# A two-model kernel on one core: gate columns in fours, one weighted sum for two norms, thirteen head products in one sequence

## The reference

```python
hc = modulate(rms_norm(ctx, norm1_g[l]), csh1, csc1)
s_ctx = bidir_delta_state(kc, vc, betac, gcx)          # 8 heads, from hc @ w_in[:, :STATE_COLS]
hx = modulate(rms_norm(x, norm1_g[l]), sh1, sc1)
y, _ = token_mixers(hx, s_ctx, w_in[l], *mix_w)        # gated delta heads + chunk MLP
x = x + gt1 * y
hx2 = modulate(rms_norm(x, norm2_g[l]), sh2, sc2)
x = x + gt2 * conv_ffn(hx2, rows, w_up[l], ffn_conv_w[l], ffn_conv_b[l], w_down[l])
...
return rms_norm(x, final_g)
```

```python
hx = _rmsnorm(x, norm_g) * (1.0 + scale_x) + shift_x
hc = _rmsnorm(ctx, norm_g) * (1.0 + scale_c) + shift_c
px = hx @ w_in
qa = _rmsnorm(hs(a_q, NA_HEADS), q_norm_a)             # each head block has its own norm
qb = _rope_2d(_rmsnorm(hs(b_q, GQA_Q_HEADS), q_norm_b), pos_row, pos_col)
...                                                     # two attentions, merge, w_out
x_new = x + gate_x * out_x
```

## Time and profile before

| | |
|---|---|
| median of three runs | 3165.26 us (3161.78 to 3167.76) |
| the profiled execution, its own time | 3160.77 us |
| span of its trace | 3159.1 us |
| PE / DVE / ACT / POOL busy | 3004.3 / 1037.8 / 727.2 / 222.5 us |
| mean granted TensorE clock | 0.981 |

### The profile page before, as it was taken

The page is one execution under the profiler, slowest core; times in us unless marked ns, Lnnn a source line. Parts: engine busy times, 40 slices in busy tenths (PEclk is TensorE's granted clock), DMA queues, the critical chain, the costliest instruction groups (busy, mean ns, idle before and its releaser), DMA issues.

```text
span 3159.1 us, 41656 instructions
## 1 busy us (share of the span) xinstructions
PE 3004.3 (95%) x16950; PEld 1726.2 (55%) x16950; DVE 1037.8 (33%) x2035; ACT 727.2 (23%) x1436; POOL 222.5 (7%) x280
## 2 busy tenths in 40 slices
PE   6999999999999999999988998999999999999998
PEld 2777767676444444444434556665555544675443
DVE  1555554554312224445211125531101212452011
ACT  3334433332200002212003224530000022362000
POOL 0222211111000000000000101000000000100000
PEclk8999999999989999999999999999999999999999
DMA  5000000002324333444331210001111112101222
GB/s 186 28 27 23 28 28 28 28 22 91 131 73 132 127 106 120 159 149 150 93 98 37 70 40 28 2 21 47 54 46 47 53 60 70 41 1 47 73 73 73
DMA packets 59846, 214.05 MB, mean 68 GB/s; under 512 B 6401, under 2 KB 8577, under 8 KB 59442
## 3 DMA queue, kind: packets, MB, share of 16 engines
q1 hardware_dynamic: 42512, 153.11, 15.3%
q0 software_dynamic: 13344, 50.59, 4.9%
...
## 4 chain that ended last, share of the span: by engine, by line
PE 90%; DVE 5%; ACT 2%; issue 2%; DMA 1%; POOL 0%; ACTq 0%; DVEq 0%
PE psum L338 87%; PE psum L704 2%; DMA arena<-in_ctxT 1%; DVE arena L1314 1%; DVE arena L1579 0%; DVE arena L1297 0%; DVE arena L1294 0%; POOL arena L1726 0%; DVE arena L1302 0%; DVE arena L1565 0%; ACT arena L942 0%; DMA arena<-in_ctx2T 0%; ACT arena L1105 0%; PE psum L534 0%; DVE psum L1571 0%
## 5 line engine op out<-in xcount | busy, mean ns | idle before, releaser
L338 PE MATMUL psum<-arena 64*64 64x64 f32 (+7 forms) x16150 | 2908.9, 363 | 143.2 <-ACT arena L875 18.4
L338 PEld LDWEIGHTS psum<-arena 128*128 128x128 f32 (+4 forms) x16150 | 1639.5, 162 | 1392.3 <-issue 1184.3
L1424 DVE SCALAR_TENSOR_TENSOR arena<-arena 128x1024 f32<-128x1024 f32 x128 | 149.3, 1221 | 4.5 <-DMA arena<-in_mods 4.4
L1672 DVE SCALAR_TENSOR_TENSOR arena<-arena,psum 128x512 f32<-128x512 f32 x32 | 21.3, 686 | 381.4 <-PE psum L338 381.4
L1105 ACT ACTIVATE arena<-psum,arena 128x512 f32<-128x512 f32 (+2 forms) x160 | 115.5, 728 | 61.3 <-DVE arena L1571 24.8
L1164 ACT ACTIVATE arena<-psum 128x512 f32<-128x512 f32 x32 | 19.1, 598 | 382.2 <-PE psum L338 382.2
L1532 DVE COPY arena<-psum 128x512 f32<-128x512 f32 (+1 forms) x26 | 18.0, 692 | 252.7 <-PE psum L338 252.7
L704 PE MATMUL psum<-arena 128*128 128x128 f32 x704 | 97.1, 282 | 2.9 <-ACT arena L1105 2.8
L704 PEld LDWEIGHTS psum<-arena 128*128 128x128 f32 x704 | 77.2, 143 | 30.6 <-issue 24.7
L1746 POOL DMA_DIRECT2D arena<-in_bias x16 | 8.8, 552 | 1193.3 <-DVE arena L1543 896.5
L1740 POOL DMA_DIRECT2D arena<-in_mods x76 | 40.3, 530 | 686.1 <-DVE arena L1424 686.1
...
## 6 DMA issues: line engine op xcount, KB each, us to landing
arena<-in_stream SPq DMA_DIRECT2D x288, 512.0 KB, 3.6
arena<-in_mods POOLq DMA_DIRECT2D x80, 512.0 KB, 3.7
...
```

The source lines that it names most:

```text
L338: return pe.matmul(out, lhsT, rhs, start=start, stop=stop, skip_group_check=True)
L1424: m = stt(mjunk[:, b % 2, :] if x < len(conds) - 1 else slot, slot, 0.5, cb[:, c, :], ALU.mult, ALU.mult, accum_out=dst(x))
```

## The change

1. **Front.** The first norm's squares go to a buffer of their own (`first_sq`); DVE adds them up (`sqsum`), and PE sums over partitions once, behind t = 13. PE waits for x and the context (`x_in`) ahead of t = 2. The gate columns are made in two groups of four tiles, first the four products of 512 columns, then the four of 256, with steps 0 to 2 of the k product behind the first group and step 3 behind the second. The first head's q product moves ahead: step 0 behind the `gcum` products, the rest behind the gate transposes. Some results change PSUM bank.
2. **Between the models.** Behind each down product DVE keeps two sums: of the squares times (final_g^2 + eps), in `sqb`, and of the plain squares, in `plain_sum`. From the first, with eps^2 in place of eps, comes the product of both roots; H is made at once from the X that is not yet normalised, with final_g in the gain (`gmod`). The second context is loaded right after the delta heads, squared by ACT in one instruction and reduced by one DVE instruction, ahead of the down products' first result. The plain root follows from one PE sum ahead of head product 1, and X is scaled by it (`last_norm`, now one tile behind each of heads 0 to 7).
3. **Heads.** All thirteen products form one sequence, each sum behind the next product; the last (`head_sum(12)`) and `rotate(3)` stand behind half of L_VB, whose context half now goes to bank 2. The wait for all rotations moves from the attention's start to the first unit that reads them.

```diff
+        plain_root = sqb[:, 0, 0:SEQ]
+        ctx_sq = flat2(mring)[:, 0:KT * CTX].rearrange("p (k n) -> p k n", k=KT)
...
                 if n in STREAMED:
-                    pe.wait_ge(s("sqsum"), (KT + 1) * (STREAMED[n] + 1))
+                    pe.wait_ge(s("sqsum"), SUMS[n])
                     m = mm(psum[:, banks[0], 0:SEQ], ones, sqb[:, 1, 0:SEQ])
                     if wide:
                         m = mm(psum[:, banks[1], 0:CTX], ones, sqb[:, 1, SEQ:TOK])
                     m.then_inc(s("nsum"), 1)
-                    return
-                for k in range(KT):
-                    norm_step(n, k, banks)
-
-            def norm_step(n, k, banks):
-
-                pe.wait_ge(s("nsq"), KT * SQUARED[n] + k + 1)
-                mm(psum[:, banks[0], 0:SEQ], ones, sqb[:, k % 2, 0:SEQ], k == 0, k == KT - 1)
-                m = mm(psum[:, banks[1], 0:CTX], ones, sqb[:, k % 2, SEQ:TOK], k == 0, k == KT - 1)
-                m.then_inc(s("nsum" if k == KT - 1 else "sq_read"), 1)
...
             for t in range(16):
                 k, hf = divmod(t, 2)
+                if t == 2:
+                    pe.wait_ge(s("x_in"), 32)
                 w = weights(pe, T_PRE + t)
                 for j in range(2):
                     r = 32 * (2 * hf + j)
                     m = mm(psum[r:r + 32, 0, :], condp[:, k, :], w[:, SEQ * j:SEQ * (j + 1)], k == 0, k == KT - 1)
                 m.then_inc(s("used"), 1)
-                if 6 <= t < 6 + KT:
-                    norm_step(0, t - 6, (1, 2))
+                if t == 13:
+                    norm_sums(0, (1, 2), True)
...
-            for k in range(KT):
-                pe.wait_ge(s("H"), k + 1)
-                r = 32 * (k % 4)
-                mm(psum[r:r + 32, 5, :], wba[:, k, :], H[:, k, 0:SEQ], k < 4, k >= 4)
-                m = mm(psum[r:r + 32, 6, 0:CTX], wba[:, k, :], H[:, k, SEQ:TOK], k < 4, k >= 4)
-            m.then_inc(s("front"), 1)
-            steps(T_HEAD, range(0, 1), 0, 1, 0)
+            for hf in range(2):
+                pe.wait_ge(s("H"), 4 * hf + 4)
+                for k in range(4 * hf, 4 * hf + 4):
+                    r = 32 * (k % 4)
+                    mm(psum[r:r + 32, 5, :], wba[:, k, :], H[:, k, 0:SEQ], k < 4, k >= 4)
+                for k in range(4 * hf, 4 * hf + 4):
+                    r = 32 * (k % 4)
+                    m = mm(psum[r:r + 32, 6, 0:CTX], wba[:, k, :], H[:, k, SEQ:TOK], k < 4, k >= 4)
+                if hf:
+                    m.then_inc(s("front"), 1)
+                steps(T_HEAD, (range(0, 3), range(3, 4))[hf], 0, 1, 0)
...
-            steps(T_HEAD, range(1, KT), 0, 1, 0)
+            steps(T_HEAD, range(4, KT), 0, 1, 0)
...
+            steps(T_HEAD + 1, range(0, 1), 4, None, 0)
             pe.wait_ge(s("gc"), 2)
...
             m.then_inc(s("gcum"), 1)
+            steps(T_HEAD + 1, range(1, KT), 4, None, 0)
...
                 if i:
                     pe.wait_ge(s("oln"), i)
-                steps(T_HEAD + 1, range(KT), 4, None, i)
+                    steps(T_HEAD + 1, range(KT), 4, None, i)
...
                 def scores(u):
                     p, q, b = us[u]
+                    if (p, q, b) == (PAIRS, 0, 0):
+                        pe.wait_ge(s("b2_rd"), 10 * l + 10)
...
+                    if u == 0:
+                        pe.wait_ge(s("b2_rs"), 5 * l + 5)
...
-                norm_sums(3 + l, (0, 1), True)
+                if l:
+                    norm_sums(4, (0, 1), True)
...
-                def heads_group(i, both):
-
...
-                            product(T0 + L_QK + j, H, 2 * (j % 2), 2 * (j % 2) + 1 if both else None, i, 4)
-                        if j:
-                            pe.wait_ge(s("b2_hsq"), 13 * l + 4 * i + j)
-                            pe.wait_ge(s("b2_hrn"), 13 * l + 4 * i + j - 1 + FREE)
-                            m = mm(psum[:, 4, :], halfones, hsq[:, (j - 1) % 2, 0:SEQ])
-                            if both:
-                                m = mm(psum[:, 5, 0:CTX], halfones, hsq[:, (j - 1) % 2, SEQ:TOK])
-                            m.then_inc(s("b2_hsum"), 1)
...
+                def head_sum(n):
+
+                    pe.wait_ge(s("b2_hsq"), 13 * l + n + 1)
+                    pe.wait_ge(s("b2_hrn"), 13 * l + n + FREE)
+                    m = mm(psum[:, 4, :], halfones, hsq[:, n % 2, 0:SEQ])
+                    if wide or n in CTX_HEADS:
+                        m = mm(psum[:, 5, 0:CTX], halfones, hsq[:, n % 2, SEQ:TOK])
+                    m.then_inc(s("b2_hsum"), 1)
+
+                for n in range(13):
+                    pe.wait_ge(s("b2_raw"), 13 * l + max(n - 1, 0) + FREE)
+                    if n == 1:
+                        pe.wait_ge(s("b2_va"), CH * l + CH)
+                        if l == 0:
+                            pe.wait_ge(s("sq"), PRODUCTS[2] + 2 * KT)
+                            mm(psum[:, 6, :], ones, plain_sum).then_inc(s("nsum"), 1)
+                    product(T0 + L_QK + n, H, 2 * (n % 2), 2 * (n % 2) + 1 if wide or n in CTX_HEADS else None)
+                    if n:
+                        head_sum(n - 1)
+                    if n >= 10:
+                        rotate(n - 10)
 
                 w = weights(pe, T0 + L_VB)
+                pe.wait_ge(s("b2_raw"), 13 * l + 12 + FREE)
                 for c in range(CH):
-                    if c == XC:
-                        pe.wait_ge(s("b2_hrn"), 13 * l + 13 + FREE)
+                    if c == 3:
+                        head_sum(12)
+                        rotate(3)
                     for k in range(KT):
-                        m = mm(psum[:, 7, (c % 4) * P:(c % 4 + 1) * P] if c < 4 else
-                               psum[:, 5, (c % 4) * P:(c % 4 + 1) * P], H[:, k, c * P:(c + 1) * P],
+                        m = mm(psum[:, 2 if c >= XC else 7, (c % 4) * P:(c % 4 + 1) * P], H[:, k, c * P:(c + 1) * P],
                                w[:, k * P:(k + 1) * P], k == 0, k == KT - 1)
                 m.then_inc(s("used"), 1)
                 rotate(4)
                 pe.wait_ge(s("b2_raw"), 13 * l + 13 + FREE)
                 pe.wait_ge(s("b2_vb"), l + 1)
-                pe.wait_ge(s("b2_qk"), 13 * l + 13 + FREE)
-                pe.wait_ge(s("b2_rd"), 10 * l + 10)
+                pe.wait_ge(s("b2_hrn"), 13 * l + 13 + FREE)
...
+            for k in range(KT):
+                if k >= 2:
+                    act.wait_ge(s("sqsum"), k)
+                f(first_sq[:, k % 2, :], X[:, k, :], ACT.Square).then_inc(s("nsq"), 1)
...
             act.wait_ge(s("ob"), HEADS + FREE)
+            act.dma_start(X[:, :, SEQ:TOK], a_ctx2).then_inc(s("b2load"), 16)
             act.dma_start(lnrows, a_lnrows.to_broadcast([P, 2, D])).then_inc(s("mixload"), 16)
...
-
+            act.wait_ge(s("b2load"), 16)
+            act.wait_ge(s("biased"), 3)
+            f(ctx_sq, X[:, :, SEQ:TOK], ACT.Square).then_inc(s("nsq"), 1)
             act.wait_ge(s("xd"), 8 + 4)
             act.dma_start(con2, a_con2).then_inc(s("b2load"), 16)
-            act.dma_start(X[:, :, SEQ:TOK], a_ctx2).then_inc(s("b2load"), 16)
...
+            norm_root(2, (0, 1), True, eps=vec("eps", 5))
...
+                if l == 0:
+                    norm_root(3, (6, None), False, to=plain_root)
+                for n in range(13):
+                    head_norm(l, n, KQ[:, n:n + 1, :] if n < 8 else bqk[n - 8])
...
+                at, done = SUMS[2] - KT, PRODUCTS[2]
+                xk, x2, gain = X[:, bass.ds(k, 1), 0:SEQ], sqb[:, 0, 0:SEQ], fgain[:, bass.ds(k, 1)]
+                dve.wait_ge(s("sqsum"), k + at)
+                dve.wait_ge(s("sq"), 2 * k + done)
+                tt(x2[:, None, :], xk, xk, ALU.mult).then_inc(s("sq"), 1)
+                dve.wait_ge(s("sq"), 2 * k + done + 1)
+                stt(sqb[:, 1, 0:SEQ], x2, gain, sqb[:, 1, 0:SEQ], ALU.mult, ALU.add).then_inc(s("sqsum"), 1)
+                tt(plain_sum, plain_sum, x2, ALU.add).then_inc(s("sq"), 1)
...
+            squares_begin(0)
+            for k in range(KT):
+                dve.wait_ge(s("nsq"), k + 1)
+                dve.wait_ge(s("sqsum"), k + 1)
+                tt(sqb[:, 1, :], sqb[:, 1, :], first_sq[:, k % 2, :], ALU.add).then_inc(s("sqsum"), 1)
...
+            tt(fgain, vec("final", 0, 8), vec("final", 0, 8), ALU.mult).then_inc(s("gate"), 1)
+            dve.wait_ge(s("gate"), 3)
+            ts(fgain, fgain, EPS, None, ALU.add).then_inc(s("gate"), 1)
+            gain_times_scale(2, vec("norm_2", 0, 8), adaT[:, 8:16, :])
+            tt(gmod[:, :, 0:1], gmod[:, :, 0:1], vec("final", 0, 8)[:, :, None], ALU.mult).then_inc(s("gmod"), 1)
             squares_begin(2)
+            dve.memset(plain_sum, 0.0)
+            dve.wait_ge(s("nsq"), KT + 1)
+            dve.wait_ge(s("sqsum"), SUMS[2] - KT - 1)
+            dve.tensor_reduce(sqb[:, 1, SEQ:TOK], ctx_sq.rearrange("p k n -> p n k"), AX_X, ALU.add)\
+                .then_inc(s("sqsum"), 1)
+            dve.wait_ge(s("gate"), 4)
...
```

(22 more changed lines are left out.)

155 lines of the change are left out of this document (49 added, 106 removed).

## The result

The changed kernel takes 3112.98 us (median of 4 runs, 3104.24 to 3118.22), the kernel before 3166.51 us (4 runs, 3161.78 to 3168.1). The ratio is 0.9831 with a 95% interval of 0.9805 to 0.9856: faster by 53.5 us, 1.7%, clear of the noise. The profiled execution has a span of 3102.4 us and a time of 3104.24, the shortest of its four. Against 3159.1 us of span before that is -56.7, where the sum of the prediction said -54.8.

The account below looks back on a forecast made before the run. PE was taken as the bound, busy 3004.3 of 3159.1 us. The terms -10.2 - 2.5 - 21.3 + 0.9 - 18.5 - 3.2 sum to -54.8, giving 3110.5 us from the median, own range 3105 to 3116 (chance 0.62).

Parts of the forecast that it names:

- A: Front: last modulation slot ends at 41.8 instead of 51.98 us, x landing at about 21; -10.2 us, bounds -13 and -0.4.
- the prediction's own signs of being wrong: Front: among these signs, slots more than 1.5 us apart behind 28 us.
- The rule weighed there: Front: PE waiting for a DMA before each small tile falls to low clock each time; -0.4 instead of -10.2 us.
- B: From T0 (DVE's first scaling of H) to the first head's kk: -2.5 us, ends 0 and -4.4.
- The new wait of 4.2 us: First head: with q moved from behind the decay rows, PE stalls 4.2 us for ACT's squares of k.
- C: Between the models, last down product to first value product: -21.3 us, ends -19 and -23.
- The plain sum: Head stage: costs PE one matmul, +0.9 us; its root and eight scalings fit behind the products.
- D: Heads: 13.4 us of PE gaps and 3 x 1.7 us of clock loss go; -18.5 us, ends -16.5 and -18.5.
- E: Attention's start: PE starts scores about 2 us earlier; -1.6 us a layer, -3.2 in all, ends 0 and -3.2.
- The clock did not hold: Rival: no half clock before the first kk or behind the gaps between the models; another -5 to -8, 3104; chance 0.14.
- the stream rival: Front: PE stays at half clock through the slots, or x lands late; gain only -0.4, so 3120 us; chance 0.15.
- The slots did not wait one at a time: Front rival: 14 slots taken singly at 5.7 us, the last ending at 101; sum +4, 3170 us; chance 0.02.

Follow-up runs that it names:

- d_groups: Changed kernel with the sums of heads 3 and 7 directly behind their own products again, in both layers: 3128.3 us.
- bias_full: Changed kernel with the mixer's row bias added by a product over all 128 partitions instead of one: 3097.93 us, ratio to the kernel before 0.9792.
- heads_only: Kernel before with the head sequence and the later attention waits alone, no plain sum: 3139.04 us, ratio to the kernel before 0.9923.
- att_wait: Changed kernel with PE held at each attention's start until the last rotated block is written, as before: 3115.86 us.
- no_plain: Changed kernel without the plain norm's work (PE sum, root, scalings) in the heads of layer 0: 3117.25 us.

## Why the prediction was right

The time, 3110.5, is 2.5 us from the median of 3112.98, and the span, 3104.3, is 1.9 us from 3102.4. Term by term, it was less exact than that:

- **A, the slots: -10.2 forecast, -7.5 measured,** and -7 to -9.5 over the executions with these slots. The landing of x (21, measured 22.0) was right, and so were the half clock behind the long wait and the hidden squares and additions. The step that was off: "Behind them the DMAs set the pace: 0.52 MB at 0.4 MB/us is 1.31 us a slot". The windows from 27 to 45 have 336, 239 and 309 GB/s, so ten slots took 27.70 to 44.49, 16.8 us instead of 13.8 (ten at 1.31 are 13.1, not the 13.3 written). That is 1.68 us a slot, and more than 1.5 was one of the prediction's own signs of being wrong: it came. About 1 us of the difference is the clock, since `d_groups` and `bias_full`, back at full pace by 32 us, end their last slot at 43.59 and 43.42; what held the stream for the rest stays open. A second size was off without effect: at half clock four slots took 3.64 us, not 2.0 each, but the next slot had not landed. The rule weighed there (the Trainium skill, "TensorE: Matmul & The Clock Gate", section "HAM oscillation") is about waits longer than the work between them. Without the wait PE waited 0.24 to 0.68 us ahead of each of the slots 9 to 13, less than the 1.05 us of a slot, and kept a granted clock of 1.00 from 21 to 33 us; the low clock in the changed kernel followed the single wait of 13.26 us.
- **B, to the first kk: -2.5 forecast, -1.1 measured, and no gain shown.** The new wait of 4.2 us on the square of k came at 4.26 and where it was said. But both ends of the forecast were mis-sized: the chain gave T0 + 52.7 for before, where the profile has T0 + 54.0, and T0 + 50.8 to 51.1 for the change, where it has T0 + 52.9. The lower clock was underrated at both (0.54 from 84 to 94 in the earlier trace rows, 0.79 from 85 to 100 in the changed kernel), and since `heads_only` passes the old order in 50.9, the 1.1 is within what the clock does from one execution to the next.
- **C, between the models: -21.3 forecast, -22.0 measured.** The value product comes 9.32 us behind the last down product, 9.0 forecast. The 1 us taken off for the clock behind C's gaps was not needed: a window at 0.56 follows (1646 to 1652), but one at 0.68 stood behind the old gap too.
- **The plain sum: +0.9 forecast, +1.0 measured** by leaving its work out. ACT's root and DVE's scalings are hidden.
- **D and E, heads and attention: -18.5 - 3.2 = -21.7 forecast.** The two layers' gain of 20.9, with the plain sum's 1.0 put back, is 21.9, and 23.2 if layer 1 is taken with the clock at its start that the kernel before had. The runs part the 23.2: 15.9 for the sums at the group ends, with the price of 1.7 us of clock behind each 2.75 measured as 1.8 in layer 0; 5.2 for the attention's start; 2.1 left for the last head's gaps of 1.89 and 1.32.
- **What the sum had no term for:** 4.57 us in the mixer, where the profiled execution of the changed kernel had the best case of a clock that varies between executions. Without it the span would have been 3107, and its median run is indeed 9 us longer than the profiled one. That the single number came out within 2 us owes something to this cancelling the 4.1 us that A and B fell short. That is luck: what was forecast well are C, D and E, which make 43 of the 54.8.

The other outcomes did not come. The clock did not hold (0.50 to 33 us). The stream was slower than forecast, but far from the 3120 of the stream rival. The slots did not wait one at a time: the largest wait of PE for a slot was 2.02 us.

A part of the rest is the clock too: from layer 1's first transposes to the end the changed kernel takes 433.6 us and the kernel before 435.8; `bias_full` and `att_wait` have 433.5 and 433.3, `no_plain` 436.3 with the same instructions there. The difference stands in the first 12 us: the granted clock is 1.00 there in the changed kernel and 0.72 in `no_plain`, as in the kernel before (rows not shown). Why it falls in one execution and not in another stays open.
